# A hybrid attention block on one core: the first tile projected row block by row block, and output products in front of the weighing

## The chip, the core and the metric

The kernel runs on one NeuronCore of a Trainium2 chip. Its engines work side by side, each through its own list of instructions in order: TensorE (PE in the profile; PEld is its loading of weights), VectorE (DVE), ScalarE (ACT), GpSimd (POOL), and SyncE (SP), which issues the transfers. They wait for each other by semaphores. The metric is the device time in microseconds (us) of one execution.

## The reference

One decoder layer over 2048 tokens, 1024 wide, fp32. Cut to what matters:

```
hn = rmsnorm(x, g_mix_pre);  z = hn @ w_in                    # w_in: 1024 x 1604
q, k, v, q_idx, k_idx, w_idx, pool_in = split(z)               # rotary on 16 dims of a head
score[t, s] = sum_h w_idx[t, h] * relu(q_idx[t, h] . k_idx[s]) # indexer, causal
keep the 256 keys of highest score for each query
attn = softmax(q.k over kept keys) @ v                         # 8 heads, 2 kv heads, dim 64
pool = (trailing mean over 2/4/8/16 - token) @ w_pool * scale
h = x + rmsnorm(concat(attn, pool) @ w_o)
h = h + rmsnorm(square(relu(rmsnorm(h) @ w_up)) @ w_down)
h = h + rmsnorm(sigmoid(h @ w_ple_gate) * (p @ w_ple_proj))
```

## The kernel before

Tokens are worked in 16 tiles of 128. There are three stages on one core, each with its own lists of instructions on every engine.

**Projection (to about 439 us).** An fp32 product is made of three products of split operands: `split_product` multiplies high by high, high by low and low by high. The weights `w_in` come from memory in eight row blocks of 128 rows (`w_in_raw[:, k, :]`); ScalarE makes the high part with the gain column `g_pre_col` as its scale (L986), VectorE the low part (L1442). For each tile `square_x` and `norm` scale x, TensorE transposes it (L1703), ScalarE and VectorE bring the high and low part of the transposed tile into `hnT_hi` (L941) and `hnT_lo` (L1267), in two halves. Then `project_to` makes four groups of columns one after the other, each in its own PSUM bank and each over all eight row blocks: 512, 512, 68 and 512 columns. ScalarE evacuates them (`evacuate_za`, `evacuate_zb`, `evacuate_zc`, `copy_pool_rows`), VectorE rotates (`rope`), and TensorE turns the pool rows (`transpose_pool`) and the keys (`transpose_k`) between the groups of the next tile. The semaphore `half_used` tells that the first four blocks of the transposed tile are used up by the last group, so that the next tile may overwrite them. The sines and cosines of the rotation come from a chain of 18 small steps on VectorE (L1242 to L1256) and one sine on ScalarE (L910); it stands ahead of everything else.

SyncE issues positions, three small columns and the pool weights, then tiles 0 and 1 of x, then the eight row blocks. They are signalled by two semaphores, one for each four row blocks.

**Attention (about 439 to 1547 us).** The work of a tile is eight heads, each over one to four blocks of up to 512 keys (one block for tiles 0 to 3, two for 4 to 7, three for 8 to 11, four for 12 to 15). A step m is one head and block; there are 320. On TensorE a step is: scores of a block two heads ahead (`score_block`, L1754 and L1755), turning the probabilities of step m + 2 (`turn_probs`, L1840), `weigh(m)` (L1854: probabilities by values, into bank 4), and the products of the indexer of later tiles (`search_part`, `index`). VectorE adds the mask and takes the maximum (`mask_block`, L1484), ScalarE exponentiates (L1058) and copies the turned probabilities to memory (L1071), for which `weigh` waits. Between these, VectorE and ScalarE run rounds of a search for the threshold of each query (`count_exact` L1346 on VectorE, `count_below` L968 on ScalarE, `move_threshold` L1363), 32 rounds for each pair of tiles, spread over the steps by a list of costs made ahead. Indexer products, transposed queries and scores share a ring of three PSUM banks; TensorE waits for a slot until VectorE has read it (`wait_ring`).

The output projection of the tile before is eight products for each half of 512 columns (L1874): four each at the end of heads 2, 3, 4 and 5. Its inputs are the transposed attention output (`transpose_o` at the end of head 1, `evacuate_oT` on ScalarE at head 2) and the pooled part, loaded by SyncE. `evacuate_mix` follows on ScalarE at heads 4 and 6.

**MLP and gate (to the end).** Weights stream through, split in high and low parts, and TensorE is nearly always busy. The change does not touch it.

Of the kernel before, what the change touches and what calls it, by code (L numbers as in the profile page):

```python
# [7 lines left out]
P = 128  # L8
F32 = mybir.dt.float32
# [38 lines left out]
def hybrid_block(nc, x, p, positions, g_mix_pre, w_in, w_pool, pool_scale, w_o, g_mix_post,  # L48
# [32 lines left out]
    with ExitStack() as ctx:  # L81
# [135 lines left out]
        w_in_ld = [sem("w_in_ld_low"), sem("w_in_ld_high")]  # L217
# [200 lines left out]

        AHEAD_BLOCKS = 2
# [142 lines left out]
        def _(sp):  # L562
            def row_over_partitions(dst, src):
                return sp.dma_start(dst, src.to_broadcast([P, D]))

            sp.dma_start(pos_i[:], positions[0].rearrange("(t p) -> p t", p=P),
                         allow_slow_non_contiguous=True).then_inc(small_ld, 16)
            for dst, src in ((g_pre_col, g_mix_pre), (pool_scale_col, pool_scale), (g_mlp_col, g_mlp_pre)):
# [4 lines left out]
            def load_x(i, u):  # L573
                sp.dma_start(x_in[:, u, :], x_tiles[i]).then_inc(x_ld[u], 16)

# [3 lines left out]

            load_x(0, 0)  # L580
            load_x(1, 1)
            for k in range(K):
                sp.dma_start(w_in_raw[:, k, :], w_in[0, k * P:(k + 1) * P, :]).then_inc(w_in_ld[k // (K // 2)], 16)
# [324 lines left out]
        def _(act):  # L908
            act.wait_ge(turns_rdy, 1)
            nc.scalar.activation(trig[:], turns[:], ACT.Sin).then_inc(trig_rdy, 1)  # L910

# [67 lines left out]
            act.wait_ge(setup_step, 4 + ROT_HALF + G)  # L979
            act.wait_ge(small_ld, 16 * 5)  # L980
            junk_early = kept_early[:, 512:1024].bitcast(BF16)
            square_x(0)
            square_x(1)
            for k in range(K):
                act.wait_ge(w_in_ld[k // (K // 2)], 16 * K // 2)
                nc.scalar.activation(w_in_hi[:, k, :], w_in_raw[:, k, :], ACT.Identity,  # L986
                                     scale=g_pre_col[:, k:k + 1]).then_inc(w_in_hi_rdy, 1)
# [3 lines left out]

            evacuate_hnT(0, 0)
            for i in range(T):
                evacuate_hnT(i, 1)
                if i >= 1:
                    copy_pool_rows(i - 1)
                if i + 2 < T:
                    square_x(i + 2)
                if i >= 1:
                    search_part(4 * i - 1, junk_early)  # L1000
                evacuate_za(i, i % 2)
                if i >= 1:
                    evacuate_pool(i - 1)
                search_part(4 * i, junk_early)
                evacuate_zb(i, i % 2)
                if i >= 1:
                    evacuate_k(i - 1)
# [223 lines left out]
        def _(dve):  # L1231
            dve.wait_ge(small_ld, 16 * 5)
            dve.wait_ge(setup_step, 4 + ROT_HALF + G)
            done = [0]

            def link(ins):
                done[0] += 1
                ins.then_inc(rot_setup, 1)
                dve.wait_ge(rot_setup, done[0])


            link(nc.vector.tensor_copy(pos_f[:], pos_i[:]))  # L1242
            link(nc.vector.tensor_tensor(angle[:], over(pos_f[:], ROT_HALF),
                                         freq[:].unsqueeze(1).to_broadcast([P, T, ROT_HALF]), ALU.mult))
            for n, (quarter, shift) in enumerate(((0.0, 0.0), (0.25, float(np.pi / 2)))):
                link(nc.vector.tensor_scalar(turns[:, n], angle[:], float(1 / (2 * np.pi)), quarter, ALU.mult, ALU.add))
                link(nc.vector.tensor_scalar(turns[:, n], turns[:, n], ROUND, None, ALU.add))
                link(nc.vector.tensor_scalar(turns[:, n], turns[:, n], -ROUND, None, ALU.add))
                rest = angle[:]
                for part in TWO_PI:  # L1250
                    link(nc.vector.scalar_tensor_tensor(out=trig[:, n], in0=turns[:, n], scalar=float(-part), in1=rest,
                                                        op0=ALU.mult, op1=ALU.add))
                    rest = trig[:, n]
                link(nc.vector.tensor_scalar(turns[:, n], trig[:, n], shift, None, ALU.add))
                link(nc.vector.tensor_scalar(turns[:, n], turns[:, n], PI_SAFE, -PI_SAFE, ALU.min, ALU.max))
            nc.vector.tensor_copy(rot[:, 0, 0:1, 0:1], turns[:, 0, 0:1, 0:1]).then_inc(turns_rdy, 1)  # L1256

# [23 lines left out]
            def rope(i, u):  # L1281
                dve.wait_ge(za_ev, i + 1)
# [153 lines left out]

            norm(0, 0)

            for k in range(K):

                dve.wait_ge(w_in_hi_rdy, k + 1)
                nc.vector.scalar_tensor_tensor(out=w_in_lo[:, k, :], in0=w_in_raw[:, k, :], scalar=g_pre_col[:, k:k + 1],  # L1442
                                               in1=w_in_hi[:, k, :].bitcast(F32), op0=ALU.mult,
                                               op1=ALU.subtract).then_inc(w_in_lo_rdy, 1)
# [3 lines left out]
            for i in range(T):  # L1448
                evacuate_hnT(i, 1)
                if i >= 1:  # L1450
                    rope(i - 1, (i - 1) % 2)
                    early_part(4 * i - 1)
# [614 lines left out]
```

## Time and profile before

| what | value |
|---|---|
| timed runs | 3245.02, 3249.56, 3249.63 us; median 3249.56 |
| the profiled execution | 3245.62 us, of which the program's span is 3243.8 |
| TensorE busy | 2958.4 us, 91% of the span |
| VectorE busy | 1719.7 us, 53% |
| ScalarE busy | 1384.8 us, 43% |
| GpSimd busy | 390.2 us, 12% |
| mean granted clock of TensorE | 0.945 |

Rows of the trace below come from the profiled execution, and times in them count from the start of its span. "x8" behind a row is the number of instructions in it; brackets hold the idle time of the engine in front and what ended it. An fp32 product that isn't split (L1874, L1854) leaves two records.

### The profile page before, as it was taken

How to read it: one execution, taken by the hardware profiler on the slowest of the kernel's cores; microseconds unless marked ns; L12 is line 12 of the kernel's file. 1: busy time of each engine (PE TensorE's matmuls, PEld its weight loads, DVE VectorE, ACT ScalarE, POOL GpSimd, SP SyncE). 2: the span in 40 equal slices, each digit the busy share in tenths (PEclk: the TensorE clock that was granted, in tenths of full speed). 3: DMA queues.
4: the chain of work that ended last, by engine and by line, in shares of the span. 5: the costliest groups of instructions: out<-in, count | busy, mean ns of one | idle time of the engine just before them, and what ended most of it. 6: DMA issues, size and time to landing. Idle time of an engine off the chain costs nothing.

```text
span 3243.8 us, 37680 instructions
## 1 busy us (share of the span) xinstructions
PE 2958.4 (91%) x14264; PEld 2407.2 (74%) x14264; DVE 1719.7 (53%) x3405; ACT 1384.8 (43%) x2202; POOL 390.2 (12%) x447
## 2 busy tenths in 40 slices
PE   5999977788788898899699999999999999999987
PEld 4887755566666676787588888888888888888875
DVE  3376778686777776832333344533445334453344
ACT  3252546575747547655322243322433224332232
POOL 1233331213040040000000001000010000100001
PEclk9999988889897887899899999999999999999998
DMA  3111142111110110111424233333323333233321
GB/s 122 61 49 54 38 126 69 36 59 44 40 50 28 41 41 11 45 33 43 149 91 134 94 117 104 117 126 102 117 97 124 124 104 117 92 130 123 103 92 39
DMA packets 224627, 266.50 MB, mean 82 GB/s; under 512 B 58176, under 2 KB 160320, under 8 KB 224448
## 3 DMA queue, kind: packets, MB, share of 16 engines
q1 hardware_dynamic: 222144, 255.72, 25.0%
q10 hardware_dynamic: 2304, 8.39, 0.6%
q8 instruction: 113, 1.85, 0.2%
q14 instruction: 66, 0.54, 0.1%
HBM read 224.07 MB, written 40.01 MB: 81 GB/s over the span
## 4 chain that ended last, share of the span: by engine, by line
PE 79%; DVE 7%; issue 7%; ACT 4%; POOL 2%; DMA 1%; SPq 0%; DVEq 0%; ACTq 0%; POOLq 0%
PE bank L1732 58%; PE bank L1874 6%; PE bank L1854 6%; PE bank L1754 3%; PE bank L1840 2%; PE bank L1755 2%; ACT kept L968 2%; DVE kept L1346 1%; PE bank L1703 1%; DVE probs L1484 1%; ACT probsT L1071 1%; POOL score L868 1%; DVE too_few L1354 1%; DMA w_in_raw<-in_w_in 1%; ACT score_tail L968 0%
## 5 line engine op out<-in xcount | busy, mean ns | idle before, releaser
L1554 DVE TENSOR_TENSOR w_lo<-w_raw,w_hi 128x1024 fp32r<-128x1024 f32 x296 | 361.5, 1222 | 582.2 <-ACT w_hi L1114 582.1
L1114 ACT CAST w_hi<-w_raw 128x1024 fp32r<-128x1024 f32 x296 | 308.5, 1043 | 661.4 <-PE bank L1732 641.5
L1854 PE MATMUL bank<-values,probsT 128*128 128x64 f32 x2176 | 335.3, 301 | 150.9 <-ACT probsT L1071 124.2
L1854 PEld LDWEIGHTS bank<-values,probsT 128*128 128x128 f32 x2176 | 314.6, 220 | 177.3 <-ACT probsT L1071 163.6
L1732 PE MATMUL bank<-hn_hi,w_hi 128*128 128x512 f32 x1024 | 400.2, 391 | 20.8 <-DVE hn_lo L1574 20.8
L1732 PE MATMUL bank<-hn_hi,w_lo 128*128 128x512 f32 x1024 | 398.9, 390 | 0.0
L1732 PE MATMUL bank<-hn_lo,w_hi 128*128 128x512 f32 x1024 | 398.9, 390 | 0.0
L1732 PE MATMUL bank<-w_hi,hid_hi 128*128 128x512 f32 x1024 | 398.7, 389 | 0.0
L1732 PE MATMUL bank<-w_hi,hid_lo 128*128 128x512 f32 x1024 | 398.4, 389 | 0.0
L1732 PE MATMUL bank<-w_lo,hid_hi 128*128 128x512 f32 x1024 | 398.4, 389 | 0.0
L1484 DVE CUSTOM_DVE_ANT_0 probs<-bank,mask 128x384 f32<-128x384 f32 (+3 forms) x320 | 193.7, 607 | 234.3 <-PE bank L1755 232.5
L968 ACT ACTIVATE kept<-score,threshold 128x1024 bf16<-128x1024 f32 (+4 forms) x160 | 251.9, 1574 | 112.2 <-DVE threshold L1363 91.8
L1346 DVE TENSOR_SCALAR_CACHE_REDUCE kept<-score,threshold 128x896 bf16<-128x896 f32 (+4 forms) x160 | 267.6, 1673 | 0.7
L1172 ACT ACTIVATE square<-bank 128x512 f32<-128x512 f32 x128 | 76.5, 598 | 405.5 <-PE bank L1732 405.4
L1874 PE MATMUL bank<-wo_sb,mixT_t 128*128 128x512 f32 x512 | 247.0, 628 | 2.2 <-ACT h_t L1036 1.1
L1630 DVE CAST hid_hi<-square 128x512 fp32r<-128x512 f32 x128 | 56.1, 438 | 360.3 <-ACT square L1174 360.3
L1732 PEld LDWEIGHTS bank<-hn_hi,w_hi 128*128 128x128 f32 x1024 | 192.6, 188 | 61.0 <-DVE w_lo L1554 21.2
L1732 PEld LDWEIGHTS bank<-hn_hi,w_lo 128*128 128x128 f32 x1024 | 192.5, 188 | 40.0
L1732 PEld LDWEIGHTS bank<-hn_lo,w_hi 128*128 128x128 f32 x1024 | 192.7, 188 | 39.5
L1732 PEld LDWEIGHTS bank<-w_hi,hid_hi 128*128 128x128 f32 x1024 | 192.2, 188 | 40.1
L1732 PEld LDWEIGHTS bank<-w_hi,hid_lo 128*128 128x128 f32 x1024 | 192.2, 188 | 39.8
L1732 PEld LDWEIGHTS bank<-w_lo,hid_hi 128*128 128x128 f32 x1024 | 192.2, 188 | 39.7
(200 smaller groups left out, 4983.1 us busy)
## 6 DMA issues: line engine op xcount, KB each, us to landing
w_raw<-in_w_up SPq DMA_DIRECT2D x64, 1024.0 KB, 5.7
w_raw<-in_w_down SPq DMA_DIRECT2D x64, 1024.0 KB, 5.0
w_raw<-in_w_ple_gate SPq DMA_DIRECT2D x16, 1024.0 KB, 5.1
x_in<-in_x SPq DMA_DIRECT2D x16, 512.0 KB, 3.6
q_t<-q_scratch SPq DMA_DIRECT2D x32, 256.0 KB, 3.7
x_t<-in_x SPq DMA_DIRECT2D x16, 512.0 KB, 4.3
h_scratch<-h_t SPq DMA_DIRECT2D x16, 512.0 KB, 2.9
hnT_scratch<-hn2T_t SPq DMA_DIRECT2D x16, 512.0 KB, 3.8
```

The source lines that it names most:

```text
L968: nc.scalar.activation(junk[:, 0:P * (t + 2)], score_of(t + 1), ACT.Sign, scale=-1.0, bias=threshold[:, 1:2].bitcast(F32), accum_out=below ...
L1114: nc.scalar.copy(piece_parts(p, w_hi[:, p % 4, :]), raw_piece(p)).then_inc(w_hi_rdy, 1)
L1172: nc.scalar.activation(square[:, f % 2, :], bank[:, UP[q % 2][f % 2], :], ACT.Relu).then_inc(relu2_step, 1)
L1346: nc.vector.tensor_scalar(junk[:, 0:P * (t + 1)], score_of(t), threshold[:, 0:1].bitcast(F32), -float(P), ALU.is_lt, ALU.add, accum_out=be ...
L1484: nc.vector.tensor_tensor_reduce(out=probs[:, H % 3, o:o + w], in0=bank[:, ring_bank[("s", H, b)], 0:w], in1=mask[:, i % 2, o:o + w], scal ...
L1554: nc.vector.tensor_tensor(piece_parts(p, w_lo[:, p % 4, :]), raw_piece(p), piece_parts(p, w_hi[:, p % 4, :]).bitcast(F32), ALU.subtract).t ...
L1732: ins = nc.tensor.matmul(dst, lhs[a], rhs[b], start=(first and n == 0), stop=(last and n == 2))
L1754: nc.tensor.matmul(dst, hi, k_parts[:, key, o:o + w], start=True, stop=False)
L1755: return nc.tensor.matmul(dst, lo, k_parts[:, key, o:o + w], start=False, stop=True)
L1840: last = nc.tensor.transpose(bank[:, 1 + m % 3, a * P:(a + 1) * P], probs[:, H % 3, o + a * P:o + (a + 1) * P], ident[:])
L1854: last = nc.tensor.matmul(bank[:, 4, h * HEAD:(h + 1) * HEAD], probsT[:, m % 3, a * P:(a + 1) * P], values[:, kt, HEAD * kv:HEAD * (kv + 1 ...
L1874: last = nc.tensor.matmul(bank[:, mix_bank(i, n), :], mixT_t[:, k, :], wo_sb[:, k, n * 512:(n + 1) * 512], start=(k == 0), stop=(k == K - 1))
```

## The change

There are two parts.

1. The start. Tile 0 of x is loaded first, then the gain column, row blocks 0 to 3, tile 1, row blocks 4 to 7, and then the positions and other small tensors. Each row block has a semaphore of its own. For the first tile alone, TensorE takes the row blocks in the outer loop and the four groups of columns in the inner one (`project_first_tile`), with the transposes of tile 1 behind block 5. The splits on ScalarE and VectorE are put between the first tile's other work. The 18 steps for the rotation angles and the sine go behind the evacuation of tile 1 on VectorE, and behind that of tile 0's groups on ScalarE.
2. The attention stage. `mix_at` deals out the products of the output projection one by one over the steps of heads 2 and 3 (first half) and 4 and 5 (second half), from the second step of the pair on. They, and `search_part`, stand in front of `weigh(m)`.

```diff
+        mix_at = {}
+        for i in range(1, T):
+            for n in range(2):
+                first = Q_HEADS * i + 2 + 2 * n
+                places = range(head_first[first] + 1, head_first[first + 2])
+                for k in range(K):
+                    mix_at.setdefault(places[k * len(places) // K], []).append((i - 1, n, k))
...
+            load_x(0, 0)
+            sp.dma_start(g_pre_col[:], g_mix_pre[0].rearrange("(k p) -> p k", p=P),
+                         allow_slow_non_contiguous=True).then_inc(g_pre_ld, 16)
+            load_w_in(range(0, K // 2))
+            load_x(1, 1)
+            load_w_in(range(K // 2, K))
             sp.dma_start(pos_i[:], positions[0].rearrange("(t p) -> p t", p=P),
                          allow_slow_non_contiguous=True).then_inc(small_ld, 16)
...
+            square_x(0)
+            act.wait_ge(g_pre_ld, 16)
+            split_weights(range(0, 1))
             evacuate_hnT(0, 0)
+            evacuate_hnT(0, 1)
+            split_weights(range(1, 4))
+            square_x(1)
+            split_weights(range(4, K))
+            evacuate_hnT(1, 0)
+            evacuate_za(0, 0)
+            evacuate_hnT(1, 1)
+            evacuate_zb(0, 0)
+            evacuate_zc(0, 0)
+            act.wait_ge(setup_step, 4 + ROT_HALF + G)
+            act.wait_ge(small_ld, 16 * 4)
+            act.wait_ge(turns_rdy, 1)
+            nc.scalar.activation(trig[:], turns[:], ACT.Sin).then_inc(trig_rdy, 1)
+            copy_pool_rows(0)
+            square_x(2)
...
             norm(0, 0)
+            dve.wait_ge(g_pre_ld, 16)
+            split_weights(range(0, 1))
+            evacuate_hnT(0, 0)
+            evacuate_hnT(0, 1)
+            split_weights(range(1, 4))
+            norm(1, 1)
+            split_weights(range(4, K))
+            evacuate_hnT(1, 0)
+            evacuate_hnT(1, 1)
+            rotations()
+            norm(2, 0)
...
+            def project_first_tile():
+
+                for k in range(K):
+                    if k % 4 == 0:
+                        pe.wait_ge(hnT_lo_rdy, k // 4 + 1)
+                    pe.wait_ge(w_in_lo_rdy, k + 1)
+                    for b, lo, hi, done_sem in ((2, 0, Z_A, za_ps), (3, Z_A, Z_B, zb_ps), (4, Z_B, Z_POOL, zc_ps), (5, Z_POOL, W_IN, zp_ps)):
+                        last = split_product(bank[:, b, 0:hi - lo], (hnT_hi[:, k, :], hnT_lo[:, k, :]),
+                                             (w_in_hi[:, k, lo:hi], w_in_lo[:, k, lo:hi]), k == 0, k == K - 1)
+                        if k == K - 1:
+                            last.then_inc(done_sem, 1)
+                    if k == 3:
+                        last.then_inc(half_used, 1)
+                    if k == 5:
+                        transpose_x(1)
...
+                for i_mix, n, k in mix_at.get(m, ()):
+                    output_projection(i_mix, n, range(k, k + 1))
+                search_part(EARLY_SPOTS + m)
                 weigh(m)
                 if m == Y_STEP:
                     pool_product(T - 1)
-                search_part(EARLY_SPOTS + m)
                 if last_of(H, b) and i >= 1:
                     if h == 1:
                         transpose_o(i - 1)
-                    if h in (2, 3):
-                        output_projection(i - 1, 0, range(4 * (h - 2), 4 * (h - 1)))
-                    if h in (4, 5):
-                        output_projection(i - 1, 1, range(4 * (h - 4), 4 * (h - 3)))
```

## Rows read from the trace of the kernel before

**Rows 1.** The page: the span, and each engine's busy time.

```profile
span 3243.8 us, 37680 instructions
...
PE 2958.4 (91%) x14264; PEld 2407.2 (74%) x14264; DVE 1719.7 (53%) x3405; ACT 1384.8 (43%) x2202; POOL 390.2 (12%) x447
```

**Rows 2.** The chain of waits over the start: start, length, what.

```profile
0.72 0.43 SPq L566
...
5.32 0.43 SPq L583
...
9.13 17.22 DMA w_in_raw<-in_w_in
...
28.04 7.29 DVE w_in_lo L1442 x4
```

**Rows 3.** Stretches of the first projection: busy by engine, clock, DMA share, GB/s.

```profile
37.50:42.70 5.20, 5.18 (x12) 4.12 (x13) 1.33 (x3) 0.00 (x0) 0.55 (x1) 1.00 0.00 0
42.70:60.40 17.70, 17.70 (x94) 14.99 (x93) 0.69 (x1) 2.35 (x7) 0.00 (x0) 1.00 0.11 31
```

**Rows 4.** Waits of 440 to 1465 us: total, times, longest.

```profile
DVE probs L1484 <- PE bank L1755: 199.4, 112, 6.9
...
PE bank L1854 <- ACT probsT L1071: 124.1, 76, 5.7
```

**Rows 5.** Timeline around one burst of output products in tile 10.

```profile
1044.30 1.11 PE L1854 MATMUL bank<-values,probsT 128*128 128x64 f32 x8 [2.06 <-ACT probsT L1071]
...
1047.77 4.58 PE L1874 MATMUL bank<-wo_sb,mixT_t 128*128 128x512 f32 x8
...
1052.85 0.69 DVE L1484 CUSTOM_DVE_ANT_0 probs<-bank,mask 128x512 f32<-128x512 f32 x1 [4.25 <-PE bank L1755]
```

**Rows 6.** Instructions on w_in_raw: landing times of its eight loads.

```profile
DMA to landing us min/median/max: 7.2/12.2/17.2
```

**Rows 7.** Instructions on x_in to 70 us: landing times of its loads.

```profile
DMA to landing us min/median/max: 3.5/5.2/10.2
```

**Rows 8.** Timeline of the start, on ScalarE, VectorE and TensorE.

```profile
0.72 1.28 ACT L910 ACT_TABLE_LOAD   x1 [0.72 <-PEq L2056]
12.12 0.42 ACT L910 ACTIVATE trig<-turns 128x256 f32<-128x256 f32 x1 [10.12 <-DVE rot L1256]
12.45 1.04 ACT L956 ACTIVATE score_tail<-x_in 128x1024 bf16<-128x1024 f32 x1
...
18.52 6.20 ACT L986 ACTIVATE w_in_hi<-w_in_raw,g_pre_col 128x1604 fp32r<-128x1604 f32 x4 [3.71 <-DMA w_in_raw<-in_w_in]
...
6.83 0.17 DVE L1242 CAST pos_f<-pos_i 128x16 f32<-128x16 int32 x1 [6.83 <-DMA w_pool_sb<-in_w_pool]
...
11.94 0.15 DVE L1256 COPY rot<-turns 128x1 f32<-128x1 f32 x1
...
61.08 0.69 DVE L1267 TENSOR_TENSOR hnT_lo<-bank,hnT_hi 128x512 fp32r<-128x512 f32 x1 [2.07 <-ACT hnT_hi L941]
...
15.41 1.94 PE L1703 MATMUL bank<-ident,x_in 128*128 128x128 f32 x8 [15.41 <-DVE x_in L1262]
```

**Rows 9.** The page's costliest groups: busy, mean ns, idle before.

```profile
L1874 PE MATMUL bank<-wo_sb,mixT_t 128*128 128x512 f32 x512 | 247.0, 628 | 2.2 <-ACT h_t L1036 1.1
```

**Rows 10.** Stretches of heads 2 to 5: tile 11; sum of tiles 1 to 15.

```profile
1133.50:1188.00 54.50, 53.32 (x281) 38.99 (x280) 34.48 (x68) 17.17 (x30) 32.48 (x27) 1.00 0.07 19
...
sum 584.60, PE 536.27 PEld 377.05 DVE 357.49 ACT 312.05 POOL 79.92; mean PE 35.75 PEld 25.14 DVE 23.83 ACT 20.80 POOL 5.33
```

**Rows 11.** Heads 2 to 5: tiles 10, 12; sum of tiles 7, 9, 10, 12.

```profile
1040.70:1093.50 52.80, 43.93 (x194) 30.33 (x193) 31.63 (x83) 33.56 (x50) 0.00 (x0) 0.84 0.05 11
1235.20:1293.60 58.40, 48.70 (x226) 36.40 (x225) 37.77 (x92) 40.04 (x55) 0.00 (x0) 0.82 0.04 10
sum 201.30, PE 168.32 PEld 118.40 DVE 125.54 ACT 129.12 POOL 6.53; mean PE 42.08 PEld 29.60 DVE 31.39 ACT 32.28 POOL 1.63
```

**Rows 12.** The stretch from tile 9's head 6 to tile 10's head 1.

```profile
998.40:1040.70 42.30, 34.53 (x169) 30.89 (x168) 35.52 (x90) 34.84 (x47) 3.46 (x3) 0.68 0.17 53
```

More of the change, by code:

```diff
@@ L214, in hybrid_block @@
         mlp_stack.close()
-        w_in_ld = [sem("w_in_ld_low"), sem("w_in_ld_high")]
+        g_pre_ld = sem("g_pre_ld")
+        w_in_ld = [sem(f"w_in_ld_{k}") for k in range(K)]
         w_in_hi_rdy = sem("w_in_hi_rdy")
@@ L1231, in _ @@
         def _(dve):
[L1232 to L1256, printed above, removed]
             def norm(i, u):
@@ L1435, in early_part @@
                 weigh_early(at["index"].get(spot, ()))
-            norm(0, 0)
[L1439 to L1444, printed above, removed]
-            norm(1, 1)
-            dve.wait_ge(trig_rdy, 1)
@@ L1447, in _, with rotations, link @@
-            evacuate_hnT(0, 0)
[L1448 to L1452, printed above, removed]
+            def rotations():
+                dve.wait_ge(small_ld, 16 * 4)
+                dve.wait_ge(setup_step, 4 + ROT_HALF + G)
+                done = [0]
+                def link(ins):
+                    done[0] += 1
+                    ins.then_inc(rot_setup, 1)
+                    dve.wait_ge(rot_setup, done[0])
+                link(nc.vector.tensor_copy(pos_f[:], pos_i[:]))
+                link(nc.vector.tensor_tensor(angle[:], over(pos_f[:], ROT_HALF),
+                                             freq[:].unsqueeze(1).to_broadcast([P, T, ROT_HALF]), ALU.mult))
+                for n, (quarter, shift) in enumerate(((0.0, 0.0), (0.25, float(np.pi / 2)))):
+                    link(nc.vector.tensor_scalar(turns[:, n], angle[:], float(1 / (2 * np.pi)), quarter, ALU.mult, ALU.add))
+                    link(nc.vector.tensor_scalar(turns[:, n], turns[:, n], ROUND, None, ALU.add))
+                    link(nc.vector.tensor_scalar(turns[:, n], turns[:, n], -ROUND, None, ALU.add))
+                    rest = angle[:]
+                    for part in TWO_PI:
+                        link(nc.vector.scalar_tensor_tensor(out=trig[:, n], in0=turns[:, n], scalar=float(-part), in1=rest,
+                                                            op0=ALU.mult, op1=ALU.add))
+                        rest = trig[:, n]
+                    link(nc.vector.tensor_scalar(turns[:, n], trig[:, n], shift, None, ALU.add))
+                    link(nc.vector.tensor_scalar(turns[:, n], turns[:, n], PI_SAFE, -PI_SAFE, ALU.min, ALU.max))
+                nc.vector.tensor_copy(rot[:, 0, 0:1, 0:1], turns[:, 0, 0:1, 0:1]).then_inc(turns_rdy, 1)
@@ L1733, in split_product, with project_to @@
                 return ins
-            def project_to(b, lo, hi, done_sem, first=False, fresh=None, half_sem=None):
+            def project_to(b, lo, hi, done_sem, fresh=None, half_sem=None):
                 for k in range(K):
```

78 lines of the change are left out of this document (39 added, 39 removed).

## The prediction, made before the changed kernel was run

> **What bounds the kernel now.** I read the page first, then the stretches of busy time, the chain of waits over the start, the timeline of the start, and last the waits of the attention stage. Everything is measured against TensorE: it is busy 2958 of 3244 us [rows 1], so only time in which it stands, or runs at its lower clock, can be won. The change touches two places.
>
> The start: the chain of waits goes through the queue of loads, the landing of the weights, two splits and then TensorE [rows 2], whose first product starts at 37.5 us. The first tile's projection then takes until 60.4 us: 5.2 us for the first 12 products (0.43 us each for 512 columns, which is the pace of 1.2 GHz) and 17.7 us for the other 84 and the 8 transposes of tile 1 [rows 3]. So 37 us pass with TensorE doing 2 us of work.
>
> The attention stage (439 to 1547 us): TensorE waits 124 us for transposed probabilities from ScalarE, and VectorE waits 199 us for scores from TensorE [rows 4]. Both stand because they stand at different moments. The timeline of one head shows it [rows 5]: TensorE waits 2.06 us before the weighing at 1044.30; 3 us later it does four output products in one go (eight records, from 1047.77, the next score at 1051.79), and VectorE stands 4.25 us until 1052.85, which makes ScalarE late for the next probabilities.
>
> **The change, part by part: the start.** Loads: tile 0 of x is issued first, at 0.72 us, the gain column next, then weight rows 0 to 3, tile 1, rows 4 to 7; the four small loads go behind them. SyncE issues the same number of transfers, in another order. In the queue of before the first weight row landed 7.2 us after its issue at 5.32, so at 12.5, and the last at 9.13 + 17.22 = 26.35 [rows 2, 6]: (26.35 - 12.5) / 7 = 1.98 us apart. New: x lands 3.5 us after issue (the shortest of its row [rows 7]), 4.2; the gain column costs about 1 us; rows of weights at 7.3, 9.2, 11.2, 13.2, tile 1 at 14.5, then 16.5 to 22.4.
>
> Tile 0: from the start of its square to the end of its transposes 17.35 - 12.45 = 4.9 us [rows 8], so 4.3 to 9.2. ScalarE splits weight row 0 from 7.3 (6.20 / 4 = 1.55 us), then copies the two halves of the transposed tile until 10.1; VectorE needs 1.82 us a row (7.29 / 4) and 0.6 us a half: row 0 until 10.8, the first half at 11.4. TensorE starts its first block at 11.4. It needs the same 5.2 + 17.7 us as before, if nothing holds it: 34.3. Does VectorE hold it? Rows 1 to 3 come at 13.9, 15.7, 17.5, tile 1's norm takes until 19.2, rows 4 to 7 come at 21.0, 22.9, 24.7 and 26.6. TensorE, at 4.5 us for the first block and 2.4 for a block at the full pace, reaches them at 15.9, 19.0, 21.4, 23.8, 26.2, 29.5 and 31.9: it is never early, and is the bound from its first product on. ScalarE's last row of weights (22.4 + 1.55) is no limit either. So the tile is done at about 34.5 instead of 60.4: 25.9 us.
>
> Given back: the 18 steps of the rotation angles on VectorE now follow the evacuation of tile 1. They take 12.09 - 6.83 = 5.26 us and the sine 0.42 [rows 8]. Tile 1's second half needs the tile before it done; its low part is ready 1.4 us behind that (61.08 + 0.69 against 60.4). Then angles, sine, and the copy of the pool rows (0.5), which ScalarE does behind the sine: 7.6 us after the end of tile 0. TensorE, in order, comes to the transpose of those rows after one projection of 24 products, 5.5 us. It stands 2.1 us, and behind it all of tile 1. What else waits (norm of tile 2, rotation of tile 0, the store of its queries) has the next projection of 5.5 us over it. Start: 25.9 - 2.1 = 24 us.
>
> The sine's function table: the trace has one table load of 1.28 us at 0.72, ahead of the sine, and none before the attention stage [rows 8]. With the square first and the sine later a second one may be placed. If it runs before ScalarE waits for the angles it costs nothing (ScalarE is idle there for some 4 us); behind that wait it adds 1.28. I take nothing and keep 1.3 for the range. The Trainium skill (ScalarE: Activation LUTs, What ACT_TABLE_LOAD costs) counts about 2.66 us for a switch, a drain included; by it, and in the wait's shadow missed, the start would give 21.3. The row of 1.28 us agrees with its figure for the load alone.
>
> Between the first tile and 439 us no order is changed, and the chain of waits shows no transfer there, so the 24 us should pass through whole. Bounds: 20 to 27; if a row of weights comes late and TensorE works the whole tile at the slow pace, see below.
>
> **The attention stage.** Nothing is added or removed. 240 of the 256 output products (0.96 us each: 247.0 us for 512 records, two to a product [rows 9]) are spread one to three a step over heads 2 to 5 of a tile, and they and the indexer's products and transposes go in front of the weighing, into TensorE's wait for the copied probabilities. Their inputs are there: ScalarE turns out the transposed mix before the copy for which the weighing waits anyway. The weighing moves back by 0.9 to 2.6 us where TensorE did not wait; behind it stand only the copy three steps on and the tile's division, so nothing is near. With one block a head (tiles 1 to 3) all eight products fall into one step: six bursts of 7 us where there were twelve of 3.5; I take 2 us lost.
>
> What there is to win: in heads 2 to 5 of all tiles TensorE is busy 536.3 of 584.6 us, so 48.3 idle [rows 10]. It is not evenly spread: tiles 7, 9, 10 and 12, where the threshold search runs, hold 33.0 of it (201.3 less 168.3 us [rows 11]), and there the granted clock is low, 0.84 in tile 10, 0.82 in tile 12 and a little more in the other two; tile 11, full of indexer products, has 1.2 us idle at clock 1.00, and gains nothing [rows 10]. Upper bound: if the products cost nothing in the search tiles, tile 10's four heads would go from 52.8 to the 42.3 of the four heads before them, which have none [rows 11, 12]; ten us each for four such tiles and a few for tiles 4 and 5 is 46. Lower bound: nothing, if the wait only moves. I take half of the idle time, 24 us, and a quarter of the lost clock (168.3 us of work x 0.15 short of full / 4 = 6), less the 2: 28 us. The waits on the two sides of a burst speak for more than nothing; that a round of the search (1.9 us on VectorE, 1.8 on ScalarE) can still be in front of a copy speaks against all. Moving the indexer's products alone I cost at nothing: they fall into stretches in which TensorE is already full.
>
> **Sum.** 24 + 28 = 52 us. The profiled execution took 3245.6 (span 3243.8), so it would take 3193.6; the median of the timed ones, 3249.6, lies 4 above, so 3197.5.
>
> **The rivals.**
> Attention unmoved: the wait for probabilities is ScalarE's round, 1.8 us ahead of a copy; filled, it comes back at the next step. For it: ScalarE's copies and rounds alternate with the threshold of VectorE. Against: VectorE is busy only 31.6 of 52.8 us there. Time: 3249.6 - 24 = 3225.5. Chance 0.17.
> All converted: bursts gone, clock up to 1.0, the 46 us and 6 more in the heads between, since indexer products reach VectorE earlier: 3249.6 - 76 = 3174. Chance 0.16.
> The start runs slow: rows arrive so that TensorE stops between blocks and stays at 0.43 us a product: 72 x 0.43 + 24 x 0.2 + 2 = 38 us instead of 22.9, 15 us lost, total 3212. Against: the rows come faster than TensorE takes them, by the sum above. The Trainium skill (TensorE: Matmul & The Clock Gate, Part 1) says that the idle state is the slow one and that activity releases it; the slow first 12 products agree, and by it this rival needs gaps. Chance 0.08.
> Slower: in front of the weighing, TensorE now stands for a PSUM slot that VectorE frees only behind a round. Place: the 39 steps with indexer products, the ring of three banks. Price: one round of VectorE, 1.94 us, where it happens, and the weighing, whose data is there, waits too. Twelve of them undo the start, 27 undo all. With nothing gained in the heads it decides from 16 on: 3249.6 - 24 + 31 = 3256.6; with all 39 it would be 3301. Chance 0.03.
>
> **How the numbers follow.** The forecast, 3185 to 3212, has 0.53; the rivals 0.17, 0.16, 0.08 and 0.03; 0.03 stays for the unforeseen. The range reaches to the first rival on one side and most of the way to the second: 3168 to 3228. Within 0.2% (6.5 us, about what a measurement of this kernel tells from no change) would need the start alone with most of it lost: 0.03. Slower 0.03, faster 0.94.
>
> **What would show it.** First product of the projection at about 11.4 us, no idle before the next ones, tile 0 done near 34.5, one wait of about 2 us at the first transpose of pool rows; the last stage the same length. In heads 2 to 5 of tiles 7, 9, 10 and 12: stretches shorter by 4 to 10 us each, granted clock over 0.9; ScalarE's share of TensorE's waits under 90 us, VectorE's wait for scores well under 199; tiles 11, 14 and 15 unchanged. The forecast is wrong if the wait for probabilities stays at 124 us with shorter single waits, or if waits for ring slots in front of the indexer's products rise above 30 us.

## The result and the profile after

The changed kernel takes 3157.4 us (median of 3 runs, 3156.5 to 3161.2) against 3249.6 before: a ratio of 0.9724, with a 95% interval from 0.9705 to 0.9743, so a gain of 83 to 96 us, 92 by the medians. The forecast was 52 us less, in a range that ended at 3168: the direction was right, the size was not, and the result lies outside the range.

The page of the changed kernel, against [rows 1] and [rows 9]:

```profile
span 3154.7 us, 37699 instructions
...
PE 2926.4 (93%) x14264; PEld 2391.6 (76%) x14264; DVE 1721.3 (55%) x3405; ACT 1384.9 (44%) x2203; POOL 390.0 (12%) x447
...
L1921 PE MATMUL bank<-wo_sb,mixT_t 128*128 128x512 f32 x512 | 242.3, 596 | 2.6 <-ACT h_t L1060 1.8
```

TensorE has the same 14264 matmuls, but 32 us less busy time; its mean granted clock went from 0.945 to 0.953. The span is 89.1 us shorter. To place that, these are the stretches of busy time with the attention stage and the last stage apart, first of the changed kernel, then of the kernel before (start:end, length, busy us of PE, PEld, DVE, ACT and POOL, granted clock, DMA share, GB/s):

```profile
412.95:1457.00 1044.05, 912.33 (x5005) 717.32 (x5006) 769.36 (x1896) 671.37 (x1119) 184.06 (x171) 0.90 0.17 50
1457.00:3154.70 1697.70, 1636.89 (x7281) 1356.53 (x7279) 705.32 (x867) 551.48 (x731) 78.75 (x51) 0.98 0.34 110
```

```profile
432.48:1547.00 1114.52, 948.20 (x5003) 736.60 (x5004) 768.50 (x1896) 672.75 (x1119) 184.11 (x171) 0.87 0.16 46
1547.00:3243.80 1696.80, 1636.03 (x7282) 1355.25 (x7280) 705.45 (x867) 551.66 (x731) 78.87 (x51) 0.98 0.34 110
```

The attention stage begins 19.5 us earlier (432.48 - 412.95) and is 70.5 us shorter (1114.52 - 1044.05); the last stage is 0.9 longer. 19.5 + 70.5 - 0.9 = 89.1. So in this trace the start came short of its 24 us, and the attention stage gave two and a half times its 28.

**The start.** The timeline of the changed kernel, on TensorE, VectorE and ScalarE:

```profile
11.41 0.80 PE L1766 MATMUL bank<-w_in_hi,hnT_hi 128*128 128x512 f32 x1 [2.02 <-DVE hnT_lo L1265]
...
40.80 0.15 DVE L1461 COPY rot<-turns 128x1 f32<-128x1 f32 x1
41.05 1.28 ACT L1017 ACT_TABLE_LOAD   x1 [5.03 <-DVE rot L1461]
42.34 0.42 ACT L1017 ACTIVATE trig<-turns 128x256 f32<-128x256 f32 x1
42.67 0.57 ACT L999 COPY zp_rows<-bank 128x512 f32<-128x512 f32 x1
...
43.29 0.66 PE L1735 MATMUL bank<-ident,zp_rows 128*128 128x128 f32 x4 [3.35 <-ACT zp_rows L999]
```

And the stretches of the same start: the first blocks, the rest of tile 0, and what comes behind it.

```profile
11.00:16.20 5.20, 4.79 (x13) 3.92 (x14) 5.09 (x5) 5.11 (x5) 0.00 (x0) 1.00 1.01 418
16.20:34.50 18.30, 18.30 (x95) 15.40 (x94) 10.15 (x8) 7.77 (x7) 0.55 (x1) 1.00 0.62 193
34.40:60.00 25.60, 22.25 (x110) 18.41 (x110) 10.49 (x32) 9.01 (x22) 8.95 (x16) 0.93 0.11 36
```

The first product starts at 11.41 us, TensorE never stands in the second row, and the tile is done at 34.4: all of that was forecast, the two times to 0.1 us. The clock column reads 1.00 in the first of these rows, as it does in [rows 3]; the trace holds no clock before 16.87 us (before 42.70 in the kernel before), and the slow pace of the first products is read from their starts, 0.43 us apart. Then comes the wait before the transpose of the pool rows, 3.35 us where 2.1 was forecast; the difference is the table load of 1.28, which stands behind the wait for the angles, not ahead of it.

**The attention stage.** Waits of the changed kernel from 400 to 1380 us (total, times, longest), against [rows 4]:

```profile
DVE probs L1517 <- PE bank L1787: 111.4, 119, 3.3
...
PE bank L1901 <- ACT probsT L1095: 90.4, 58, 5.6
...
ACT kept L979 <- DVE threshold L1362: 69.1, 78, 3.1
```

VectorE's wait for scores went from 199 to 111 us, its longest from 6.9 to 3.3; TensorE's for probabilities from 124 to 90; and ScalarE's for the threshold of the search from 91.8 to 69.1. These windows leave out the last 80 us of the stage. Over the whole of it VectorE waited, before and after,

```profile
DVE probs L1484 <- PE bank L1755: 232.5, 134, 6.9
...
DVE probs L1517 <- PE bank L1787: 142.9, 138, 3.3
```

and TensorE's waits are the same 124 and 90. The timeline of tile 10 shows how, against [rows 5]:

```profile
984.81 1.88 PE L1921 MATMUL bank<-wo_sb,mixT_t 128*128 128x512 f32 x4
...
985.84 0.46 ACT L1095 COPY probsT<-bank 128x384 f32<-128x384 f32 x1
...
986.53 1.00 PE L1901 MATMUL bank<-values,probsT 128*128 128x64 f32 x8
...
987.34 0.48 PE L1786 MATMUL bank<-k_parts,q_hi 128*128 128x512 f32 x1
...
988.09 0.69 DVE L1517 CUSTOM_DVE_ANT_0 probs<-bank,mask 128x512 f32<-128x512 f32 x1 [0.87 <-PE bank L1787]
```

ScalarE's copy for the weighing ends at 986.30, while TensorE is still at two output products (984.81 to 986.69); the weighing at 986.53 has no wait, the next score follows it at once, and VectorE stood 0.87 us where it stood 4.25. Heads 2 to 5 of tiles 7, 9, 10 and 12 of the changed kernel, against [rows 11], and the sum of all 15 such stretches, against [rows 10]:

```profile
769.00:800.10 31.10, 29.07 (x153) 20.15 (x151) 26.85 (x73) 26.93 (x42) 0.00 (x0) 1.00 0.11 26
902.10:939.20 37.10, 35.11 (x187) 24.59 (x186) 29.30 (x72) 26.95 (x42) 5.51 (x6) 1.00 0.07 16
978.40:1017.00 38.60, 35.83 (x194) 24.74 (x193) 31.74 (x83) 33.80 (x49) 0.00 (x0) 1.00 0.07 16
1156.40:1202.30 45.90, 42.62 (x226) 31.18 (x224) 37.66 (x90) 37.03 (x53) 0.00 (x0) 0.92 0.07 18
sum 152.70, PE 142.63 PEld 100.66 DVE 125.55 ACT 124.71 POOL 5.51; mean PE 35.66 PEld 25.17 DVE 31.39 ACT 31.18 POOL 1.38
...
sum 521.50, PE 505.34 PEld 360.49 DVE 360.36 ACT 314.81 POOL 76.35; mean PE 33.69 PEld 24.03 DVE 24.02 ACT 20.99 POOL 5.09
```

All heads 2 to 5: 584.6 us became 521.5, which is 63 less. Idle time fell from 48.3 to 16.2, by 32; busy time for the same products from 536.3 to 505.3, by 31. Most of these 31 are clock: weighted with the granted clock, the same busy time is worth 505 us at full clock before and 500 after, so some 26 are the clock and 5 are products that follow each other more closely. Three of the four tiles now run at granted clock 1.00 (2.4 GHz), where they had 0.91, 0.87 and 0.84. The other 7 us came in the heads between, 6 and 7 of one tile and 0 and 1 of the next (470 to 462 over all of them, to the last weighing).

### The profile page after: what moved, and what is told of

Its sections match the earlier page's. It is cut to its first block, busy times and chain, and to the rows that moved or that the text cites. A ratio compares the mean times of both kernels' runs of the same rounds, so it can differ in the third digit from the quotient of the medians.

```text
span 3154.7 us, 37699 instructions
## 1 busy us (share of the span) xinstructions
PE 2926.4 (93%) x14264; PEld 2391.6 (76%) x14264; DVE 1721.3 (55%) x3405; ACT 1384.9 (44%) x2203; POOL 390.0 (12%) x447
## 3 DMA queue, kind: packets, MB, share of 16 engines
q1 hardware_dynamic: 222144, 255.72, 25.7%
## 4 chain that ended last, share of the span: by engine, by line
PE 77%; DVE 8%; issue 6%; ACT 5%; POOL 2%; DMA 1%; DVEq 0%; ACTq 0%; POOLq 0%; SPq 0%
PE bank L1766 58%; PE bank L1901 5%; PE bank L1921 4%; PE bank L1786 3%; PE bank L1887 2%; PE bank L1787 2%; ACT kept L979 2%; DVE kept L1345 1%; PE bank L1735 1%; DVE probs L1517 1%; POOL score L882 1%; ACT probsT L1095 1%; ACT probs L1082 1%; ACT score_tail L979 1%; DVE too_few L1353 1%
## 5 line engine op out<-in xcount | busy, mean ns | idle before, releaser
L1901 PE MATMUL bank<-values,probsT 128*128 128x64 f32 x2176 | 322.6, 294 | 115.6 <-ACT probsT L1095 90.4
L1766 PE MATMUL bank<-hn_hi,w_hi 128*128 128x512 f32 x1024 | 400.2, 391 | 20.9 <-DVE hn_lo L1607 20.9
L979 ACT ACTIVATE kept<-score,threshold 128x1024 bf16<-128x1024 f32 (+4 forms) x160 | 252.0, 1575 | 94.8 <-DVE threshold L1362 69.1
L1517 DVE CUSTOM_DVE_ANT_0 probs<-bank,mask 128x384 f32<-128x384 f32 (+3 forms) x320 | 193.9, 607 | 144.2 <-PE bank L1787 142.9
L1766 PEld LDWEIGHTS bank<-hn_hi,w_hi 128*128 128x128 f32 x1024 | 192.7, 188 | 60.9 <-DVE w_lo L1587 21.2
```

The costliest lines, as they stand in the source:

```text
L979: nc.scalar.activation(junk[:, 0:P * (t + 2)], score_of(t + 1), ACT.Sign, scale=-1.0, bias=threshold[:, 1:2].bitcast(F32), accum_out=below ...
L1517: nc.vector.tensor_tensor_reduce(out=probs[:, H % 3, o:o + w], in0=bank[:, ring_bank[("s", H, b)], 0:w], in1=mask[:, i % 2, o:o + w], scal ...
L1766: ins = nc.tensor.matmul(dst, lhs[a], rhs[b], start=(first and n == 0), stop=(last and n == 2))
L1901: last = nc.tensor.matmul(bank[:, 4, h * HEAD:(h + 1) * HEAD], probsT[:, m % 3, a * P:(a + 1) * P], values[:, kt, HEAD * kv:HEAD * (kv + 1 ...
```

## The experiments

All ratios are against the kernel before, with 95% intervals; the gaps in us are between medians. Each diff is against the changed kernel. Its loop over the steps reads, behind the score blocks and transposes of each step:

```
 for i_mix, n, k in mix_at.get(m, ()):
     output_projection(i_mix, n, range(k, k + 1))      # single products
 search_part(EARLY_SPOTS + m)                          # indexer
 weigh(m)
```

**Which part gives what: the start alone, and the attention stage alone.** For the first the loop is that of before, with bursts of four and the indexer behind `weigh`; for the second the loads, splits and project loops of before are put back.

```
-                for i_mix, n, k in mix_at.get(m, ()):
-                    output_projection(i_mix, n, range(k, k + 1))
-                search_part(EARLY_SPOTS + m)
                 weigh(m)
+                search_part(EARLY_SPOTS + m)
...
+                    if h in (2, 3):
+                        output_projection(i - 1, 0, range(4 * (h - 2), 4 * (h - 1)))
```

> The changed kernel with the attention stage's order of before: four output products at a time at the end of heads 2 to 5, they and the indexer's work behind the weighing. Only the start stays changed. If the start is worth what its trace shows (19.5 us at the first transposes of the queries), this gives 3230 us, 0.994 of before. If the start and the attention stage help each other, it differs from that by more than 6 us.

> The kernel before with only the attention stage changed. If the two parts are independent, 3249.6 - 70 = 3180 us (0.978 of before); with the start-only kernel the two gains add up to the 92 us of both within 5 us.

Start alone: 3224.8 us, 0.9930 (0.9915 to 0.9944), 23.5 us less. Attention alone: 3177.3, 0.9786 (0.9768 to 0.9804), 71.5 less. Together 95, against 92 for both: the parts add up within what the runs tell apart. The surplus over the forecast is all in the attention stage.

**Which edit of the attention stage gives it: place, spreading, the indexer.** Four more orders of the same work, all with the new start.

```
 e2: weigh(m), search_part, single products
 e3: single products, weigh(m), search_part
 e4: search_part, weigh(m), single products
-                for i_mix, n, k in mix_at.get(m, ()):
-                    output_projection(i_mix, n, range(k, k + 1))
+                if last_of(H, b) and i >= 1 and h in (2, 3, 4, 5):     # e5: bursts of four, in front
+                    output_projection(i - 1, h // 2 - 1, range(4 * (h % 2), 4 * (h % 2 + 1)))
```

> The changed kernel with output products dealt out one by one over the same steps, but behind the weighing, and the indexer's work behind it as before too. Theory A (the gain comes from filling TensorE's wait for the copied probabilities, so the place in front of the weighing is what counts): spreading alone gives under a third of the 70 us of the attention stage, 3205 us or more. Theory B (the gain comes from the bursts of four being gone, which had starved VectorE of scores for 4 us each; the place within the step counts little): at least 50 of the 70 us stay, 3180 us or less.

> The changed kernel with the indexer's transposes and products behind the weighing again; the single output products stay in front. Theories A and B: no change beyond 5 us, 3153 to 3163, since indexer work falls into stretches in which TensorE is full. Theory C (the indexer's products in front bring VectorE its work earlier and are a good part of the gain): 3170 us or more.

> The changed kernel with the single output products behind the weighing and the indexer's work in front of it. Theory A: most of the attention stage's gain is lost, 3200 us or more. Theory B: 3157 to 3175 us. With the run in which both stand behind, it says what the indexer's place is worth when the products are behind.

> The changed kernel with the output products four at a time, in the last step of heads 2 to 5 as before, but in front of the weighing; indexer work in front too. Theory A (filling the wait counts): a burst of 3.5 us still covers the longest wait of a head, half or more of the 70 us stays, 3195 us or less. Theory B (the bursts themselves cost): VectorE still gets no scores for 4 us after each burst, under 20 of the 70 us stay, 3210 us or more.

| output products | indexer | us | ratio (95%) | heads 2 to 5, tiles 4 to 12 |
|---|---|---|---|---|
| bursts, behind (e1) | behind | 3224.8 | 0.9930 (0.9915 to 0.9944) | 395 us |
| single, behind (e2) | behind | 3214.7 | 0.9898 (0.9884 to 0.9913) | 362 |
| single, behind (e4) | in front | 3209.3 | 0.9885 (0.9866 to 0.9904) | 360 |
| bursts, in front (e5) | in front | 3185.8 | 0.9812 (0.9791 to 0.9832) | 358 |
| single, in front (e3) | behind | 3170.4 | 0.9765 (0.9750 to 0.9779) | 329 |
| single, in front (changed kernel) | in front | 3157.4 | 0.9724 (0.9705 to 0.9743) | 326 |

The last column (sums of the stretches of the traces) separates the two edits: spreading alone gives 33 us there, the place in front with the indexer 37, both 69. They add. Of the place, the output products' is the larger part: with single products it gives 33 (362 to 329), the indexer's 1 (e2 to e4) to 3 (e3 to the changed kernel). In the timed medians of e2 spreading seems worth only 10, because singles behind the weighing lose 21 us in tiles 1 to 3 (91 against 70), where one block a head puts all eight products of a half into one step; in front the same bunches cost 4 (73.5), and 11 against the bursts in front (62.2). The indexer's place, costed at nothing, is worth 13 with the singles in front (3170.4 to 3157.4). Few of them are in heads 2 to 5, as the last column tells, but in the heads between, which take 477 us in e3 and 462 in the changed kernel, at a mean clock of 0.77 and 0.81.

Against what was expected: the numbers of theory A, the place in front, came in e2, e4 and e5. In e3 they did not: 3170.4 us just reaches the 3170 of theory C, by which the indexer's place is a part of the gain.

**Is the smaller gain of the start the table load?** Angles and sine one place earlier on both engines, ahead of tile 1's second half.

```
             evacuate_hnT(1, 0)
+            act.wait_ge(turns_rdy, 1)
+            nc.scalar.activation(trig[:], turns[:], ACT.Sin).then_inc(trig_rdy, 1)
             evacuate_za(0, 0)
...
             evacuate_hnT(1, 0)
+            rotations()
             evacuate_hnT(1, 1)
-            rotations()
```

> The changed kernel with the 18 angle steps put in front of tile 1's evacuation on VectorE, which stands idle from 26.5 to 29.6 and from 30.9 to 35.1 us, and the sine in front of the evacuation of tile 0's first group on ScalarE. If the wait of 3.35 us at the first transpose of pool rows and the slow clock behind it (one projection of 24 products in 7.09 instead of 5.54 us) are what the start gives back, it gains 4 to 5 us on the changed kernel, 3152 to 3153. If tile 1's first half comes too late by it (VectorE needs until about 32.5, TensorE wants it at 34.4), it gains nothing.

3152.6 us, 0.9706 (0.9690 to 0.9722), 4.8 below the changed kernel; the intervals overlap, the trace decides. The stretch behind tile 0 of this kernel, and its table load:

```profile
34.40:60.00 25.60, 25.60 (x133) 21.53 (x132) 7.16 (x20) 8.92 (x23) 8.90 (x16) 1.00 0.16 52
```

```profile
31.70 1.28 ACT L1013 ACT_TABLE_LOAD   x1 [2.29 <-DVE rot L1461]
```

The load still takes 1.28 us, now under tile 0's products; TensorE has no idle time in the stretch, the clock is 1.00, and the transposes of the pool rows of every tile but the last come 26.1 to 26.4 us earlier than in the kernel before, where the changed kernel has 20.9 to 21.2 in tiles 1 to 7. That is the whole of 60.4 - 34.4 = 26.0. The attention stage then begins 24.9 us earlier, against 19.5.

**Does the loop of the heads set the pace?** If so, the score blocks belong in front of the weighing too: they lead the way back to ScalarE's copy.

```
-                for next_H, c in score_at[m]:
-                    score_block(next_H, c)
...
                 search_part(EARLY_SPOTS + m)
+                if m + 1 < len(steps):
+                    for next_H, c in score_at[m + 1]:
+                        score_block(next_H, c)
                 weigh(m)
```

> The changed kernel with the scores of step m + 1 in front of the weighing of step m too, so that what VectorE needs next never stands behind TensorE's wait for ScalarE's copy. Theory D (what counts is the loop copy, weighing, next scores, mask, threshold, round, next copy: work behind the weighing lengthens it, work in front runs beside it): the weighing itself, 0.8 to 1.8 us a step, leaves the loop as the products did; in some 150 steps of search tiles at 0.2 us or more this gives 30 us, 3127 us or less. Theory E (only idle time of TensorE filled with products counts; what is left of it comes from ScalarE and VectorE being full): within 10 us of 3157.

The score block that stood right behind a weighing now stands right in front of it. 3139.6 us, 0.9669 (0.9654 to 0.9683): 17.8 less than the changed kernel, between the two numbers given: 3127 us or less was named for the loop as the whole pace, within 10 us of 3157 for idle time alone. Waits of this kernel over its whole attention stage, 392 to 1437 us, where the changed kernel has 142.9 and 90.4 over its own:

```profile
DVE probs L1517 <- PE bank L1787: 91.3, 77, 2.9
PE bank L1901 <- ACT probsT L1095: 80.4, 59, 5.2
```

Both fall again, by 52 and 10. So the order in the loop is worth time with nothing added or taken away, but less than a loop that sets the whole pace would give.

> Scores in front of the weighing and the angle steps early, on the changed kernel. The two lie in different stages: the sum of the two gains within 3 us, 4.8 us under the kernel with the scores in front alone.

With the earlier angles as well: 3132.3 us, 0.9647 (0.9633 to 0.9662), 7 below e8: the two edits add.

**What do the output products cost in each place?** 180 of the 240 are left out (`for k in ks` becomes `for k in (x for x in ks if x in (0, K - 1) or i == T - 1)`), in the changed kernel, in e2 and in e1, whose orders are single in front, single behind and bursts behind.

> Leaves out six of the eight products of each half of the output projection (tiles 0 to 14; the first and the last are kept), 180 products in all; the rest is the changed kernel, products in front. At the full pace a product is 0.86 us of TensorE, 155 us in all. In the tiles without search rounds (3, 6, 8, 11 and 13 to 15) TensorE is full and they are worth their whole time, 84 x 0.86 = 72 us; in the eight others (96 products) Theory D says that in front they cost under a third, 25 us: together 97 us, 3060 us. If they cost as much as anywhere, 3002 us.

> The same 180 products left out of the kernel with single products and the indexer's work behind the weighing (3214.7 us). Theory D: behind the weighing products cost their full time or more, so this loses at least 155 us, 3060 us or less, and most of the 57 us between products behind and in front of the weighing disappear with the products (what stays is the indexer's place, some 13 us). If the place in front is good for something else than the products, the two kernels without them still differ by 40 us.

> The start-only kernel (bursts of four behind the weighing, 3224.8 us) without the same 180 products. Products behind the weighing cost 0.49 us each when single, 0.33 in front. In bursts they should cost more, since VectorE starves behind each: over 0.55 us each, 100 us in all, 3125 us or less, so that all three kernels without products lie within 30 us. If 3150 us or more, the burst is no dearer than a single product behind.

| order | with | without 180 | price | of one |
|---|---|---|---|---|
| single, in front | 3157.4 | 3098.0 (0.9541, 0.9527 to 0.9555) | 59 us | 0.33 |
| single, behind | 3214.7 | 3127.2 (0.9623, 0.9607 to 0.9639) | 88 | 0.49 |
| bursts, behind | 3224.8 | 3117.8 (0.9595, 0.9581 to 0.9610) | 107 | 0.59 |

By the intervals each price is good to some 7 us. None costs its full time, so the 155 us and more of the theory that the loop alone sets the pace is wrong as a whole; and in front they cost 59, not the 97 that it gave there. Nor does the place matter for these products alone: without the 180, the kernel with everything behind is still 29 us slower than the one with everything in front (3127.2 against 3098.0), half of the 57 between them with all products. The indexer's place (13 us) and the 60 products that are left (60 x 0.16 = 10 us) make most of that. By stretches it is plainer. Heads 2 to 5 of the same four tiles, in the kernel without the products:

```profile
741.90:772.30 30.40, 22.54 (x128) 17.22 (x126) 26.23 (x69) 26.76 (x42) 0.00 (x0) 0.89 0.11 27
876.80:917.10 40.30, 30.61 (x164) 24.10 (x163) 29.25 (x72) 27.92 (x43) 5.54 (x6) 0.83 0.08 19
958.00:996.10 38.10, 30.79 (x170) 23.69 (x169) 31.58 (x83) 34.00 (x52) 0.00 (x0) 0.87 0.08 17
1124.30:1170.50 46.20, 37.83 (x201) 31.11 (x201) 38.15 (x94) 38.47 (x53) 0.00 (x0) 0.82 0.06 13
sum 155.00, PE 121.77 PEld 96.12 DVE 125.22 ACT 127.15 POOL 5.54; mean PE 30.44 PEld 24.03 DVE 31.31 ACT 31.79 POOL 1.38
```

155.0 us without 48 of the products, 152.7 with them: they are free. TensorE stands 33.2 us instead of 10.1, and what it does runs at clock 0.82 to 0.89 instead of 0.92 to 1.00. Over the six search tiles (4, 5, 7, 9, 10, 12) the changed kernel takes 204.8 us and 201.0 without 72 products: 3.8 us, 0.05 each. In the old order the same six, first with and then without:

```profile
sum 267.30, PE 223.56 PEld 155.74 DVE 166.59 ACT 171.98 POOL 7.03; mean PE 37.26 PEld 25.96 DVE 27.76 ACT 28.66 POOL 1.17
```

```profile
sum 211.00, PE 162.63 PEld 128.68 DVE 165.82 ACT 167.81 POOL 6.50; mean PE 27.11 PEld 21.45 DVE 27.64 ACT 27.97 POOL 1.08
```

56.3 us for 72, 0.78 each; single but behind it is 236.2 less 220.8, 0.21 each. In the full tiles 6, 11, 14 and 15, where TensorE hardly stands, the place is no help: 173.3 against 134.1 us in the changed order, 0.82 each, and 177.2 against 135.9 with bursts behind, 0.86 each. The advantage over the bursts lies in the tiles in which TensorE had gaps to fill.

**Is it the work in the gaps that gives time, through the clock?** The kernel e8 with 98 first score products done twice, in heads 6, 7, 0 and 1 of tiles 4 to 12, where no output products lie.

```
+                if again:
+                    nc.tensor.matmul(bank[:, ring_bank[("s", H, b)], 0:w], q_hi[:, i % 2, h, :], ..., start=True, stop=True)
```

> The kernel with the scores in front of the weighing, and in heads 6, 7, 0 and 1 of tiles 4 to 12 the first product of each score block is made twice (the same values into the same bank, so nothing else changes). Some 100 products of 0.2 to 0.4 us, about 30 us of useless work, in the heads in which TensorE is idle 100 us and its granted clock is 0.83 on average. Theory D (the loop through ScalarE and VectorE sets the time of these heads): the extra lies just ahead of what VectorE waits for, so it costs 0.1 to 0.3 us each, 3145 to 3165 us. Theory F (it is the lower clock that makes these heads long, and any work that keeps TensorE going pays): clock over 0.9 in these heads, 3135 us or less.

3140.9 us, 0.9665 (0.9649 to 0.9681), against 3139.6 without. The repeated ones in the groups of this kernel:

```profile
L1876 PE MATMUL bank<-k_parts,q_hi 128*128 128x512 f32 (+1 forms) x98 | 48.6, 496 | 3.8 <-DVE block_max L1517 3.5
```

The runs can't tell the two kernels apart. Records overlap their neighbours, so the 48.6 us overstate what was added; weighted with the granted clock, TensorE's work in heads 6, 7, 0 and 1 rose by 18 us at full clock (287 to 305). Its busy time there rose by only 8 (350 to 358), for the clock rose from 0.83 to 0.86; the idle time fell from 102 to 98 us, and the length went from 452 to 455. Neither of the two numbers came, nor the clock over 0.9. The added work was paid for mostly by the faster clock; it brought no time by itself.

**The best order found**: e9, and tile 3 with its first heads used too, four products to a step (`places` starts at `head_first[first]` for it).

> Scores in front and early angles, and in tile 3 alone (one block a head, full of indexer products) the output products four a step in heads 2 to 5 in place of eight a step in heads 3 and 5. In the run with bursts in front tile 3 took 54.6 us against 60.2: some 4 us gain, 3128 us. If it is noise of that tile, 3132.

3130.9 us, 0.9636 (0.9619 to 0.9652). Tile 3's four heads go from 33.2 to 29.7 us in the traces, which is the 4 that was expected there, but the 1.4 us from e9 is within what the runs tell apart. Either is some 25 us better than the change as made.

## Why the prediction was wrong in size

**The start** was right in mechanism, point for point, up to the end of tile 0. The term was 24 us; it measured 23.5 alone, and 19.5 in the trace of the changed kernel. That the 23.5 lie so near is in part luck: the attention stage begins 22.5 us earlier in the trace of e1, where tiles 2 to 7 are hardly earlier than in the changed kernel, and traces with the same start differ by up to 4 us here. The 25.9 us of the tile held (26.0). What it gives back was mis-sized: not 2.1 us but some 5. One part is "I take nothing" for the table load, which cost 1.28 us, since it is issued behind the wait for the angles; the other is the clock behind the stall, a term that the prediction does not have: the 24 products behind it took 7.1 us in place of 5.5 (below). e7 takes both away, and 26 us arrive at the next tiles.

**The attention stage** is the failed step: "I take half of the idle time, 24 us, and a quarter of the lost clock", with 46 as an upper bound. Measured: idle time 32, busy time of the same products 31 (most of it clock), other heads 7, together 70. So the step that failed is the size of these two terms, and the bound set over them.

The idle term was short by a quarter (24 of 32). In the four tiles that I named it fell by 23 of 33 us. The reason is the loop that I described but did not follow to its end. From ScalarE's copy the way goes over the weighing, the next score on TensorE, and mask and maximum on VectorE, to the next copy. Work that TensorE does between weighing and score lengthens this way; in front of the weighing it runs beside the copy. That place and spreading each matter is shown (e1, e2, e5, the changed kernel: 395, 362, 358, 326 us), and so is that the products become nearly free in the search tiles (0.78 each down to 0.05). That it is this loop is supported by e8, where a change of order alone gives 17.8 us, but its whole price did not come in e8, e10 or e11.

The clock term was off by a factor of four to five: 26 to 31 us instead of 6. I took a quarter of the lost clock though half the idle time was to go. In the four tiles the busy time fell from 168.3 to 142.6 us, by 25.7: the whole of the 168.3 x 0.15 = 25 us, not a quarter. In these heads nearly all of it came back (0.94 to 0.99 over the 15 stretches), and e10 shows the reverse: take the products out, and the same stretches fall to 0.82 to 0.89.

The upper bound was no bound. I took the four heads that have no output products, 42.3 us in [rows 12], for what tile 10's four would be with free products; they came to 38.6. Those four heads carry other work and show no floor for these: VectorE is busy 35.5 us in them. The same heads of tile 10 without 12 of their 16 products take 38.1 us in the changed order (e10; VectorE is busy 31.6) and 40.0 in the old one (e14). The low clock of [rows 12], 0.68, is not shown to be the reason, for in e12 such heads did not get shorter as their clock rose.

"Moving the indexer's products alone I cost at nothing" was wrong by 13 us. My reason, that they fall into full stretches, does not hold for the heads between, where most of it lies; and even the full heads 2 to 5 of tiles 6 and 11 take 95.7 us in e3 and 91.1 in the changed kernel. The loss of 2 us in tiles 1 to 3 was right (71.3 to 73.5).

Of the signs, two missed: TensorE's wait for probabilities came to 90.4 us, not under 90, and the stretches of tiles 9, 10 and 12 are 12.5 to 14.2 us shorter, not 4 to 10. Tile 7 (8.4), the clock over 0.9 and the unchanged tiles 14 and 15 came; tile 11 fell from 54.5 to 52.9.

**The rivals.** Attention unmoved is excluded by e6. The slow start did not come: rows of weights landed some 2 us apart (ScalarE's last four splits, which waited for them, start at 16.68, 18.66, 20.63 and 22.95 us) and TensorE had no gap in tile 0. "Slower" did not come either: TensorE's waits for VectorE to read a slot of the ring (<- block_max, weighed and score) are 4.8 us in the attention stage before and 6.8 after, far from the 30 named. "All converted" had the right reasons, bursts gone and clock up to 1.0, and also 6 us in the heads between (7 came); its 76 us was the nearest, still 16 short, by the same false bound. Its 3174 lies inside the range of 3168 to 3228, so the result missed a range that took in even this rival.

**Left open.** How the gain divides between a shorter loop and a faster clock: the two move together in every run. e8 gained without added work, and e12 raised the clock with added work and no gain, but no run holds one fixed. Open too is the rest of the 29 us that the order gives without the 180 products.

## What to carry to other kernels

In an in-order queue, put work that nobody waits for at once in front of a wait on another engine, in small pieces, and not between that wait and what the other engine waits for next: here 180 such products cost 107 us in bursts behind the wait, 88 singly behind it and 59 singly in front. In sizing such a change, count the clock that comes back in the stretches whose gaps are filled, and take the bound from the same steps with the work left out (38.1 us here), not from steps beside them that do other work (42.3). When a function is moved, look up on which side of its wait the table load falls.

## What the runs showed of the hardware

The granted clock fell behind one short stall. After the 3.35 us in which TensorE stood before 43.29, the records from 44.30 on start 0.43 us apart (1.2 GHz) until 47.3, and from 47.66 on 0.23 us apart (2.4 GHz). Some eight products at the slow pace cost 1.5 us. This agrees with the Trainium skill (TensorE: Matmul & The Clock Gate, Part 1), by which the idle state is the slow one and activity releases it.

A table load behind an idle ScalarE cost its own row and no more: 41.05 + 1.28 = 42.33, and the sine starts at 42.34. The Trainium skill (ScalarE: Activation LUTs, What ACT_TABLE_LOAD costs) counts about 2.66 us for a switch with its drain; here nothing was in flight to drain, and no run shows that second part.

In stretches where TensorE waits for others, its work is nearly free in both directions: with 48 products taken out four stretches took 2.3 us more (155.0 against 152.7), and the 98 repeated ones of e12 made the kernel no slower that the runs can tell (3140.9 against 3139.6).
